# Two transformer blocks on one core: one modulation group summed on VectorE during the input projection, smaller bias rows, and another order of the attention copies

## The chip, the cores and the metric

The kernel runs on one core of a Trainium2 chip. The metric is device time in microseconds (us) of one execution, the median of several runs. All tensors are float32.

## The reference, cut to what matters

Batch is 1, there are 256 tokens and the model width is 1024. `first_block` is a transformer block with two kinds of attention and a gated feed-forward; `second_block` is a Hyena and HGRN mixer followed by a mixture of 16 experts, whose 403 MB of weights are read once. The change lies in the first block:

```python
mod = (silu(c) @ w_ada + b_ada)                 # (1, 6144): a 1024 x 6144 matrix times one vector
shift1, scale1, gate1, shift2, scale2, gate2 = split(mod, 6)
hn = rms_norm(h, norm1_g) * (1 + scale1) + shift1
proj = hn @ w_in                                # 1024 x 3072: q, k, v of both attentions
qa, ka, qb, kb = rms_norm of each head of 64
s = q @ k.T * Dh**-0.5 + bias[rel]              # bias: 12 heads, by relative distance key - query
o = softmax(s) @ v                              # 8 windowed heads, 4 differential heads (p1 - lam * p2)
h = h + gate1 * (o @ w_out)
hn = rms_norm(h, norm2_g) * (1 + scale2) + shift2   # then the feed-forward, gated by gate2
```

## The kernel before

The program is written engine by engine (`block.sync`, `block.gpsimd`, `block.scalar`, `block.vector`, `block.tensor`). Each engine runs its list in the order of the text, and semaphores join them (`reached` and `again` are waits on shared semaphores). Weights stream through `ring`, eight slots of 1 MB. SyncE (SP) issues the load of unit n as soon as unit n-7 is used up (`unit_done`), so the order of `units_of()` is the order of the weights: 8 units `ada` (first third of `w_ada`), 12 units `win` (`w_in`), 16 units `ada` (the other two thirds), 4 units `wout`, and so on.

**Modulation.** A unit `ada` is a 128 x 2048 tile of `w_ada`. `mod_products(m)` (L1720) makes four matmuls of it with the 32 times repeated silu(c) as weights; eight units make one group of 2048 values: group 0 is shift1 and scale1, group 1 gate1 and shift2, group 2 scale2 and gate2. ScalarE copies a finished group out of PSUM (`copy_mod_rows`, L688), TensorE turns it into columns (`mod_columns`, L1741) and VectorE adds `b_ada` (`first_mods`). The second block's modulation is made in another way: GpSimd loads tiles into the arena (`ada_load`, L595), VectorE adds them up scaled by silu(c) (`ada_sum`: the first by a `tensor_scalar`, L1292, the others by a `scalar_tensor_tensor`, L1294), and `mod_fold` sums the result over the partitions with four matmuls.

**First projection** (about 35 to 139 us). TensorE multiplies the 12 units `win` (L1775, L1786, about 7 us each). Between them lie the Hyena filters' spectra (L1764, L1765), which need `filter_halves` (L1102, L1104) on VectorE, and the norms of the heads: `sum_heads`, `head_inverse` (L1110, L1111), ScalarE's root, `spread_heads` (L1803), `head_scales` (L1119). `unmask_bias` (L1092) adds the window mask to the bias tiles just before the last `head_scales`. The bias tiles come from `t12`, 12 rows of 512 values: SP stores each row 128 times in a DRAM scratch (L518), and ScalarE's queue loads them back skewed, a row shifted by one for each partition (L755). Vector instructions stand here in the order `head_inverse(0)`, `head_scales(0)`, `filter_halves(0)`, `filter_halves(1)`, `head_inverse(1)`, `unmask_bias`, `head_scales(1)`.

**Attention** (about 139 to 185 us), 16 pairs p: two windowed heads for 128 queries each (p below 8) or the two maps of one differential head. Each engine has its own loop over p:

```python
# TensorE                      # VectorE                 # ScalarE
scores(p + 2)      # L1851     pair_inverse(p)           two Exp of pair p          # L774
mod_products(10+p) # L1720     pair_max(p + 2) # L1164   (p > 8) scale of p - 1     # L780
turn_probs(p)      # L1864     pair_out(p - 2) # L1187   copy of turned p - 2       # L787
pv(p - 1)          # L1878, L1874                        (some p) mod rows, context squares # L762
```

There are two buffers for scores and exponentials, but one PSUM bank for the turned probabilities (`PTB`) and one tile for the outputs (`PVB`): `turn_probs(p)` waits for ScalarE's copy of p-1, and `pv(p-1)` for VectorE's `pair_out(p-2)`. `mod_products(8)` and `(9)` stand ahead of the loop and `(10)` to `(23)` in its first 14 steps. Then follow `w_out`, the feed-forward (a seven-product scheme with sums on GpSimd and VectorE), the second block's mixers, and the experts.

Of the kernel before, what the change touches and what calls it, by code (L numbers as in the profile page):

```python
# [91 lines left out]
         "up_copied": ("qk_raw", 8), "ada2_landed": ("counts_landed", 16)}  # L92
# [3 lines left out]
def units_of():  # L96

    u = [("ada", i) for i in range(8)] + [("win", i) for i in range(12)] + [("ada", i) for i in range(8, 24)]
    u += [("wout", i) for i in range(4)] + [("ada2", m) for m in NORM2_FILL]
    for i in range(FT // 2):  # L100
        u += [("wup", i)] + ([("cin", CTX_U[0])] if i == FT // 2 - 1 else []) + [("wup", FT // 2 + i)]
        u += [("ada2", m) for m in WUP_FILL.get(i, ())]
    for i in range(FT // 2):
        u += [("wdn", i)]
        u += [("cin", CTX_U[CTX_FILL[i]])] if i in CTX_FILL else []
    u += [("ada2", m) for m in NORM3_FILL]
    u += [("win2", i) for i in WIN2]
    u += [("wout2", i) for i in range(4)]
    return u
# [119 lines left out]
def two_blocks_kernel(nc, a, out):  # L229

    rel_dram = nc.dram_tensor("rel_scratch", (12, P, 512), F32).ap()
# [17 lines left out]
    with ctx:  # L249
# [63 lines left out]

        awide, asum = (at(8, 2048), at(16, 2048), at(0, 2048)), at(82, 2048)
# [50 lines left out]
        def mod_rows(g):  # L365

            if g == 0:
                return X[:, 1, :], HI[:, 1, 0, :]
            return (L[:, 2, :], modrA) if g < 3 else (X[:, 1, :], modrB)
# [112 lines left out]
        def _(sp):  # L482
# [16 lines left out]
            for n, (kind, i) in enumerate(units):  # L499
                if n >= RING:  # L500
                    sp.wait_ge(S["unit_done"], n - RING + 1)
                if kind == "wdn":
                    src = a["w_down"].rearrange("l (k p) n -> p (l k) n", p=P)[:, 2 * i:2 * i + 2, :]
                    dst = slot(n).rearrange("p (k n) -> p k n", k=2)
                elif kind in ("ada", "ada2"):
                    q, k = i // KT, i % KT
                    src = a[UNIT_SRC[kind]][0, k * P:k * P + P, 2048 * q:2048 * q + 2048]
                    dst = slot(n)
                else:
                    src = a[UNIT_SRC[kind]][i, :, :]  # L510
                    dst = slot(n)
                sp.dma_start(dst, src).then_inc(S[f"slot{n % RING}_landed"], 16)
                if n == upos[("wdn", 1)] + RING:
                    sp.wait_ge(S["ffn_act"], FT // 2)
                    expert_pair(0)
                if n == 16:
                    out_of_bank(sp, "rel")
                    sp.dma_start(rel_dram, t12[0:12, :].unsqueeze(1).broadcast_to([12, P, 512])).then_inc(S["rel_stored"], 16)  # L518
# [40 lines left out]
        def _(pool):  # L559
# [10 lines left out]
            load(hc[:, :, :], a["p_ctx"], "ctx_landed")  # L570
# [8 lines left out]

            pool.wait_ge(S["rel_stored"], 16)  # L580
# [4 lines left out]

            pool.wait_ge(S["scores_done"], 16)
# [65 lines left out]
        def _(act):  # L652
# [26 lines left out]
            def copy_mod_rows(g):  # L679

                if g == 4:
                    act.wait_ge(S["ada_folded"], 1)
# [49 lines left out]
            for i in range(12):  # L732
# [19 lines left out]
                if i == 7:  # L752
                    act.wait_ge(S["rel_stored"], 16)
                    act.wait_ge(S["qk_ready"], 4)
                    act.dma_start(biasW[:, :, :], bass.AP(tensor=rel_dram.tensor, offset=P, ap=[[511, P], [512 * P, 12], [1, T + P]])  # L755
                                  ).then_inc(S["bias_landed"], 16)

            def context_squares(i):

                act.wait_ge(S["unit_done"], upos[("win", 11)] + 1)  # L760
                act.wait_ge(S["ctx_landed"], 16)
                sq = A(hn[:, 2 * i:2 * i + 2, :], hc[:, 2 * i:2 * i + 2, :], ACT.Square)  # L762
                if i == 3:
                    sq.then_inc(S["ctx_sq"], 1)

            NP_ = 16
            for p in range(NP_ + 2):
# [20 lines left out]
                if p in (6, 15):  # L788
                    copy_mod_rows(1 if p == 6 else 2)
# [200 lines left out]
        def _(dve):  # L990
# [98 lines left out]
            def unmask_bias():  # L1089
                dve.wait_ge(S["bias_landed"], 16)  # L1090
# [3 lines left out]
            def filter_halves(o):  # L1094
                for i, h in ((0, HR), (2, HI)):
# [8 lines left out]
                    done(V.tensor_tensor(h[:, o, 1, :], e_, o_, ALU.subtract), "lin_emptied_by_dve")  # L1104

# [176 lines left out]
            def ada_sum(j):  # L1282
# [5 lines left out]
                if k == 0 and j:  # L1288
                    dve.wait_ge(S["ada_folded"], 1)
# [216 lines left out]
            dve.wait_ge(S["masks_landed"], 16)  # L1506
# [47 lines left out]
            dve.wait_ge(S["router_landed"], 16)  # L1554
# [98 lines left out]
        def _(pe):  # L1653
# [54 lines left out]
            def mod_products(m):  # L1708
# [5 lines left out]
                if m in (0, 8):  # L1714
                    pe.wait_ge(S["cond_repeated"], 1 if m == 0 else 3)
                if k == 0 and g >= 1:
                    pe.wait_ge(S["mod_rows_copied"], g)
# [6 lines left out]
            def mod_fold(g):  # L1724

                pe.wait_ge(S["ada_summed"], KT if g == 4 else len(SUMMED))
                pe.wait_ge(S["mod_rows_copied"], g)
                for c in range(4):
                    last = MM(mod_rows(g)[0][32 * c:32 * c + 32, :], ones[:, 0:32], asum[:, c * 512:c * 512 + 512],
                              start=True, stop=(g == 4), skip_group_check=True)  # L1730
# [433 lines left out]
            pe.wait_ge(S["dft_landed"], 16)  # L2164
# [244 lines left out]
```

## Time and profile before

| | us |
|---|---|
| median of 3 runs | 1596.08 (1594.73 to 1596.18) |
| profiled execution, its own time | 1595.4 |
| its span | 1593.6 |
| busy in it: TensorE / VectorE / ScalarE / GpSimd | 1230.3 / 435.8 / 223.5 / 143.7 |

A page of the profile gives the busy time of each engine, the same in 40 slices of the span, the chain of work that ended last (followed back from the last instruction, each step to what released it), and groups of instructions by line. The trace behind it can be asked for stretches of time, for one tile, and for who waited for whom. PE is TensorE (PEld its weight loads), DVE VectorE, ACT ScalarE, POOL GpSimd, SP SyncE; SPq, ACTq and POOLq rows are issues of DMAs. Times of rows count from the start of the span.

### The profile page before, as it was taken

The numbers are of one execution on the slowest core, as the hardware profiler recorded it, in microseconds if no ns is written. First come the engines' busy times: TensorE is split into PE (matmuls) and PEld (weight loads), VectorE is DVE, ScalarE is ACT, GpSimd is POOL, SyncE is SP. The second block draws the span as 40 slices with busy tenths as digits, with TensorE's granted clock in tenths as the row PEclk, the third lists the DMA queues.
The fourth block names the chain that finished last, engine by engine and source line by source line (L and its number), as shares of the span: only waits on it lengthen the run. The fifth ranks groups of instructions, "written<-read, shape, count | busy, mean of one in ns | idle before, by whom it ended". The sixth has DMA issues, their size and how long they took to land.

```text
span 1593.6 us, 17838 instructions
## 1 busy us (share of the span) xinstructions
PE 1230.3 (77%) x7618; PEld 691.6 (43%) x7618; DVE 435.8 (27%) x894; ACT 223.5 (14%) x458; POOL 143.7 (9%) x143
## 2 busy tenths in 40 slices
PE   7999999999999999987665655555566666666555
PEld 4775579998888789842111111111111111111111
DVE  4635756775443577320000000000000000000001
ACT  2224522232103321120000000000000000000001
POOL 1100046650000031000000000000000000000000
PEclk9999999999999999999888897888886887788888
DMA  9886765457953335789999999999999999999997
GB/s 387 234 269 267 304 264 212 170 175 304 411 180 132 132 110 186 312 343 428 428 429 428 428 430 427 429 428 428 429 427 429 429 428 429 427 429 428 428 428 299
DMA packets 53414, 545.29 MB, mean 342 GB/s; under 512 B 5884, under 2 KB 7932, under 8 KB 14300
## 3 DMA queue, kind: packets, MB, share of 16 engines
q1 hardware_dynamic: 47724, 521.69, 80.8%
q0 software_dynamic: 3200, 18.43, 2.9%
q10 hardware_dynamic: 2416, 4.07, 0.7%
q8 instruction: 60, 0.98, 0.2%
q14 instruction: 14, 0.11, 0.0%
HBM read 539.97 MB, written 4.19 MB: 341 GB/s over the span
## 4 chain that ended last, share of the span: by engine, by line
PE 50%; DMA 40%; another core or an unknown queue 4%; DVE 3%; ACT 1%; issue 1%; SPq 0%; ACTq 0%; DVEq 0%
DMA arena<-in_exp_w_dram 22%; DMA ring<-in_exp_w_dram 12%; PE L L1936 8%; PE L L2101 7%; DMA tok<-in_exp_w_dram 6%; PE X L2320 6%; PE L L2048 5%; PE L L1775 4%; PE X L2348 3%; PE X L1995 3%; PE L L1786 2%; PE L L2220 2%; PE L L1921 2%; PE L L1720 1%; PE L L2361 1%
## 5 line engine op out<-in xcount | busy, mean ns | idle before, releaser
L2320 PE MATMUL X<-arena,side 128*32 128x512 f32 x1280 | 193.1, 734 | 123.6 <-DMA arena<-in_exp_w_dram 123.6
L2320 PEld LDWEIGHTS X<-arena,side 128*32 128x32 f32 x1280 | 39.7, 122 | 269.7 <-DMA arena<-in_exp_w_dram 195.7
L1609 DVE TENSOR_TENSOR side<-side,X 128x512 f32<-128x512 f32 x16 | 11.0, 687 | 496.8 <-ACT side L972 496.8
L2320 PE MATMUL X<-ring,side 128*32 128x512 f32 x512 | 82.9, 779 | 66.4 <-DMA ring<-in_exp_w_dram 66.4
L2348 PE MATMUL X<-ring,side 128*32 128x512 f32 x512 | 75.9, 721 | 53.2 <-DMA ring<-in_exp_w_dram 53.2
L2101 PE MATMUL L<-tok,ring 128*128 128x256 f32 x448 | 99.4, 379 | 0.3 <-ACT tok L808 0.3
L2101 PEld LDWEIGHTS L<-tok,ring 128*128 128x128 f32 x448 | 84.3, 190 | 13.9 <-issue 3.1
L642 POOL TENSOR_TENSOR side<-side 128x256 f32<-128x256 f32 x16 | 9.8, 615 | 871.0 <-DVE side L1619 808.2
L1614 DVE TENSOR_TENSOR side<-X,side 128x512 f32<-128x512 f32 x16 | 11.1, 692 | 281.0 <-PE X L2348 281.0
L972 ACT ACTIVATE side<-X 128x512 f32<-128x512 f32 x16 | 9.6, 597 | 513.3 <-PE X L2320 513.3
L2048 PE MATMUL L<-arena,ring 128*128 128x256 f32 x352 | 77.4, 379 | 0.3 <-DVE arena L1349 0.3
L2320 PEld LDWEIGHTS X<-ring,side 128*32 128x32 f32 x512 | 16.0, 126 | 130.5 <-DMA ring<-in_exp_w_dram 101.2
L2048 PEld LDWEIGHTS L<-arena,ring 128*128 128x128 f32 x352 | 66.6, 190 | 9.7 <-DVE arena L1349 0.7
L2348 PE MATMUL X<-tok,side 128*32 128x512 f32 x256 | 44.3, 806 | 32.9 <-DMA tok<-in_exp_w_dram 32.9
L2348 PEld LDWEIGHTS X<-ring,side 128*32 128x32 f32 x512 | 15.7, 124 | 115.8 <-DMA ring<-in_exp_w_dram 88.4
L1936 PE MATMUL L<-arena 128*128 128x128 f32 x528 | 63.3, 275 | 1.4 <-DVE L L1320 1.2
L1936 PEld LDWEIGHTS L<-arena 128*128 128x128 f32 x528 | 61.0, 192 | 1.8 <-DVE L L1320 1.4
L2348 PE MATMUL X<-arena,side 128*32 128x512 f32 x256 | 49.1, 907 | 11.9 <-ACT side L976 7.6
L1775 PE MATMUL L<-tok,ring 128*128 128x256 f32 x256 | 56.6, 381 | 0.7 <-ACT tok L700 0.7
L1775 PEld LDWEIGHTS L<-tok,ring 128*128 128x128 f32 x256 | 48.3, 190 | 10.4 <-issue 3.1
L970 ACT ACTIVATE side<-X 128x256 f32<-128x256 f32 x16 | 6.1, 383 | 312.7 <-PE X L2294 312.7
L2361 PE MATMUL L<-side 64*128 64x512 f32 x128 | 38.9, 731 | 13.9 <-DVE side L1614 13.9
(399 smaller groups left out, 1652.9 us busy)
## 6 DMA issues: line engine op xcount, KB each, us to landing
arena<-in_exp_w_dram SPq DMA_DIRECT2D x96, 2048.0 KB, 50.2
ring<-in_exp_w_dram SPq DMA_DIRECT2D x64, 2048.0 KB, 50.1
ring<-in_w_in_dram SPq DMA_DIRECT2D x34, 1024.0 KB, 5.1
more<-in_exp_w_dram SPq DMA_DIRECT2D x15, 2048.0 KB, 49.7
tok<-in_exp_w_dram SPq DMA_DIRECT2D x15, 2048.0 KB, 49.1
ring<-in_w_ada_dram SPq DMA_DIRECT2D x24, 1024.0 KB, 9.3
ring<-in_w_up_dram SPq DMA_DIRECT2D x22, 1024.0 KB, 4.9
arena<-in_ada_w_dram POOLq DMA_DIRECT2D x15, 1024.0 KB, 9.8
```

The lines of the kernel that those rows point to most:

```text
L1720: last = MM(mod_rows(g)[0][32 * c:32 * c + 32, :], cond, slot(n)[:, c * 512:c * 512 + 512], start=(k == 0), stop=(k == KT - 1), skip_group ...
L1775: last = MM(L[:, j % 4, m * T:m * T + T], w[:, k, m * P:m * P + P], src(k), start=(k == 0), stop=(k == KT - 1))
L1786: last = MM(L[:, j % 4, t * T:t * T + T], src[:, k, t * P:t * P + P], w[:, k, :], start=(k == 0), stop=(k == KT - 1))
L1921: last = MM(L[:, j % 4, m * T:m * T + T], w[:, k, m * P:m * P + P], oT[:, k, :], start=(k == 0 and m == 0), stop=(k == KT - 1), skip_group ...
L1936: last = MM(out, w[:, k, :], x(k), start=(first and k == 0), stop=True, skip_group_check=True)
L1995: last = MM(bank[:, x * T:x * T + T], wk, hk, start=(k == 0), stop=(k == KT - 1))
L2048: return MM(L[:, pos["wdn"][m // 2] % 4, (m % 2) * T:(m % 2) * T + T], w[:, kk, m * P:m * P + P], aT[:, 2 * i + kk, :], start=(i == 0 and ...
L2101: last = MM(L[:, j % 4, x * T:x * T + T], wk, hk, start=(k == 0), stop=(k == KT - 1))
L2220: last = MM(L[:, j % 4, m * T:m * T + T], w[:, k, m * P:m * P + P], yTh[:, k, :] if k < HG else yTg[:, k - HG, :], start=(k == 0 and m == ...
L2320: last = MM(X[CAP * j:CAP * j + CAP, w, :], xe[:, k % 2, k // 2, :], v, start=(k == 0), stop=(k == KT - 1))
L2348: last = MM(X[CAP * b:CAP * b + CAP, 2, :], hTe[:, 2 * x + c, CAP * j:CAP * j + CAP], w[:, nb * 512:nb * 512 + 512], start=(u == 16), stop ...
L2361: MM(XB[2 * t + n], ge[h0:h0 + HD, t, :], ys[h0:h0 + HD, :], start=False, stop=True, skip_group_check=True).then_inc(S["scatter_done"], 1)
```

## The change

Eight units `ada`, those of group 1, leave the ring. GpSimd's queue loads them during the first projection into free parts of the arena and of `more`, and VectorE adds them up with silu(c) into `hc` (where the context was loaded before). One fold of four matmuls takes the place of group 1's 32 at the start of the attention, and group 2's eight products stand in the even steps of TensorE's loop only. The context is loaded later, after the fold. The scratch rows are stored 32 times, and ScalarE's queue issues four loads of 32 partitions each. `pair_out(p-2)` moves ahead of `pair_max(p+2)`. Copying and turning group 1 move to steps 2, 4 and 7. Groups 1 and 2 have PSUM banks of their own. Four semaphores are used twice, which only changes counts in other waits (left out below).

```diff
-    u = [("ada", i) for i in range(8)] + [("win", i) for i in range(12)] + [("ada", i) for i in range(8, 24)]
+    u = [("ada", i) for i in range(8)] + [("win", i) for i in range(12)] + [("ada", i) for i in range(16, 24)]
...
-    rel_dram = nc.dram_tensor("rel_scratch", (12, P, 512), F32).ap()
+    rel_dram = nc.dram_tensor("rel_scratch", (12, 32, 512), F32).ap()
...
+        first_wide = (more[:, 256:2304], at(8, 2048), at(78, 2048), more[:, 256:2304], at(20, 2048), at(32, 2048), more[:, 256:2304], at(40, 2048))
+        first_sum = hc.rearrange("p k t -> p (k t)")
...
             pool.wait_ge(S["slot7_landed"], 16)
-            load(hc[:, :, :], a["p_ctx"], "ctx_landed")
+            def first_load(j):
+                pool.dma_start(first_wide[j], a["w_ada"][0, j * P:j * P + P, 2048:4096]).then_inc(S[f"first{j % 4}_landed"], 16)
+            for j in range(3):
+                first_load(j)
             load(dftE[:, :, :, :], a["k_dft"][:, 0:2, :, :], "dftE_landed")
             load(cntW[:, :], a["k_logcnt"], "counts_landed")
...
+            again(pool, "first_summed", 1)
+            first_load(3)
+            reached(pool, "filt_ready")
+            first_load(4)
             pool.wait_ge(S["rel_stored"], 16)
...
+            again(pool, "first_summed", 4)
+            first_load(6)
+            pool.wait_ge(S["HF_done"], 8)
+            pool.wait_ge(S["HN_done"], 2)
+            first_load(5)
+            first_load(7)
+            pool.wait_ge(S["ada_folded"], 1)
+            load(hc[:, :, :], a["p_ctx"], "ctx_landed")
             pool.wait_ge(S["scores_done"], 16)
...
+                if u == 4:
+                    again(act, "first_summed", 2)
                 A(qk[:, u, :, :].rearrange("p m t -> p (m t)"), L[:, j % 4, :], ACT.Copy).then_inc(S["qk_raw"], 1)
...
                 if i == 7:
                     act.wait_ge(S["rel_stored"], 16)
                     act.wait_ge(S["qk_ready"], 4)
-                    act.dma_start(biasW[:, :, :], bass.AP(tensor=rel_dram.tensor, offset=P, ap=[[511, P], [512 * P, 12], [1, T + P]])
-                                  ).then_inc(S["bias_landed"], 16)
+                    again(act, "first_summed", 3)
+                    for g in range(4):
+                        act.dma_start(biasW[32 * g:32 * g + 32, :, :],
+                                      bass.AP(tensor=rel_dram.tensor, offset=P - 32 * g, ap=[[511, 32], [512 * 32, 12], [1, T + P]])
+                                      ).then_inc(S["bias_landed"], 16)
...
-                if p in (6, 15):
-                    copy_mod_rows(1 if p == 6 else 2)
+                if p in (2, 15):
+                    copy_mod_rows(1 if p == 2 else 2)
...
+            def first_add(n):
+                j = (0, 1, 2, 3, 4, 6, 5, 7)[n]
+                again(dve, f"first{j % 4}_landed", 16 * (j // 4 + 1))
+                if n:
+                    again(dve, "first_summed", n)
+                    done(V.scalar_tensor_tensor(first_sum, first_wide[j], csil[:, j:j + 1], first_sum, ALU.mult, ALU.add), "first_summed")
+                else:
+                    done(V.tensor_scalar(first_sum, first_wide[j], csil[:, j:j + 1], None, ALU.mult), "first_summed")
...
             head_inverse(0)
+            for j in range(3):
+                first_add(j)
             head_scales(0)
             filter_halves(0)
+            first_add(3)
+            first_add(4)
             filter_halves(1)
+            for n in range(5, KT):
+                first_add(n)
             head_inverse(1)
             unmask_bias()
             head_scales(1)
...
+                if p >= 2:
+                    pair_out(p - 2)
                 if p + 2 < 16:
                     pair_max(p + 2)
-                if p >= 2:
-                    pair_out(p - 2)
-                if p == 11:
+                if p == 7:
                     first_mods(1)
...
-            mod_products(8)
-            mod_products(9)
+            mod_fold(1)
+            mod_products(16)
             for p in range(17):
                 if p + 2 < 16:
                     scores(p + 2)
-                if p < 14:
-                    mod_products(10 + p)
+                if p < 14 and p % 2 == 0:
+                    mod_products(17 + p // 2)
                 if p < 16:
                     turn_probs(p)
-                if p == 8:
+                if p == 4:
                     mod_columns(1)
```

## Rows read from the trace of the kernel before

**Rows 1.** The page: the chain that ended last, by engine

```profile
PE 50%; DMA 40%; another core or an unknown queue 4%; DVE 3%; ACT 1%; issue 1%; SPq 0%; ACTq 0%; DVEq 0%
```

**Rows 2.** Stretches: length, busy PE, PEld, DVE, ACT, POOL (instructions), clock, DMA share, GB/s

```profile
109.00:122.00 13.00, 13.00 (x62) 11.45 (x61) 0.15 (x1) 2.15 (x4) 0.00 (x0) 1.00 0.90 335
150.00:161.00 11.00, 11.00 (x96) 5.16 (x96) 7.30 (x36) 6.54 (x22) 0.00 (x0) 1.00 1.01 423
```

**Rows 3.** The chain through the attention: start, us, what

```profile
138.83 1.06 PE X L1851 x8
...
148.40 0.59 PE L L1864 x4
148.98 0.59 PE L L1878 x8
149.58 0.63 PE X L1851 x4
150.21 1.00 PE L L1720 x8
...
173.64 0.37 PE L L1864 x2
174.02 0.68 PE L L1874 x4
...
184.84 3.69 PE L L1921 x16
```

**Rows 4.** The timeline of one step, windowed heads: start, us, engine, line

```profile
149.51 0.70 PE L1851 MATMUL X<-arena 64*128 64x256 f32 x4
...
150.26 0.42 DVE L1164 CUSTOM_DVE_ANT_0 arena<-X,arena 128x256 f32<-128x256 f32 x1 [0.91 <-PE X L1851]
...
151.27 0.51 ACT L774 ACTIVATE arena<-arena,small 128x256 f32<-128x256 f32 x1 [1.24 <-DVE small L1167]
...
152.27 0.57 ACT L787 ACTIVATE arena<-L 128x512 f32<-128x512 f32 x1
```

**Rows 5.** The same timeline in the differential heads: ScalarE's end of a step

```profile
172.48 0.36 ACT L787 ACTIVATE arena<-L 128x256 f32<-128x256 f32 x1
...
172.75 0.62 ACT L762 ACTIVATE tok<-tok 128x512 f32<-128x512 f32 x1
```

**Rows 6.** The timeline of VectorE in the first projection, with the idle time before each

```profile
80.90 3.35 DVE L1111 RECIPROCAL arena<-arena 128x512 f32<-128x512 f32 x1
91.66 2.72 DVE L1119 SCALAR_TENSOR_TENSOR arena<-arena,small,X 128x512 f32<-128x512 f32 x4 [7.42 <-PE X L1803]
...
106.15 0.69 DVE L1102 TENSOR_TENSOR side<-L,side 128x512 f32<-128x512 f32 x1 [8.97 <-ACT side L708]
...
127.07 0.69 DVE L1110 TENSOR_SCALAR arena<-X 128x512 f32<-128x512 f32 x1 [17.92 <-PE X L1796]
...
131.06 3.29 DVE L1092 TENSOR_TENSOR arena<-arena 128x3072 f32<-128x3072 f32 x1
135.31 2.72 DVE L1119 SCALAR_TENSOR_TENSOR arena<-arena,small,X 128x512 f32<-128x512 f32 x4 [0.95 <-PE X L1803]
```

**Rows 7.** The arena's groups on VectorE, 370 to 500 us: ns min/median/max, starts

```profile
L1294 DVE SCALAR_TENSOR_TENSOR arena<-arena,small x13: 2350/2352/2353, 378.4 to 437.5; 128x2048 f32<-128x2048 f32 x13
...
L1292 DVE TENSOR_SCALAR arena<-arena,small x2: 1281/1284/1286, 377.0 to 416.0; 128x2048 f32<-128x2048 f32 x2
```

**Rows 8.** DMA issues: what, queue, count, KB each, median us to landing

```profile
arena<-in_ada_w_dram POOLq DMA_DIRECT2D x15, 1024.0 KB, 9.8
...
arena<-rel_scratch ACTq DMA_DIRECT2D x1, 2304.0 KB, 12.6
```

**Rows 9.** GpSimd and SyncE around the bias store, from their timelines

```profile
95.65 0.40 POOL L582 COPY arena<-small 128x256 f32<-128x256 f32 x1 [37.76 <-DMA rel_scratch<-arena]
...
47.95 0.94 SPq L518 DMA_DIRECT2D rel_scratch<-arena  x1
```

**Rows 10.** Waits of TensorE on the input weights, 34 to 140 us: us, times, longest

```profile
PEld L L1775 <- DMA ring<-in_w_in_dram: 1.0, 1, 1.0
```

More of the change, by code:

```diff
@@ L91 @@
          "up_top": ("qk_inv", 2), "up_right": ("max_ready", 16), "up_corner": ("qk_ready", 8),
-         "up_copied": ("qk_raw", 8), "ada2_landed": ("counts_landed", 16)}
+         "up_copied": ("qk_raw", 8), "ada2_landed": ("counts_landed", 16), "first0_landed": ("ctx_landed", 0), "first1_landed": ("router_landed", 0),
+         "first2_landed": ("masks_landed", 0), "first3_landed": ("dft_landed", 0), "first_summed": ("xT_done", 4)}
 CHAIN_OF = {step: chain for chain, steps in CHAINS.items() for step in steps}
 def units_of():
-    u = [("ada", i) for i in range(8)] + [("win", i) for i in range(12)] + [("ada", i) for i in range(8, 24)]
+    u = [("ada", i) for i in range(8)] + [("win", i) for i in range(12)] + [("ada", i) for i in range(16, 24)]
     u += [("wout", i) for i in range(4)] + [("ada2", m) for m in NORM2_FILL]
@@ L368, in mod_rows @@
                 return X[:, 1, :], HI[:, 1, 0, :]
-            return (L[:, 2, :], modrA) if g < 3 else (X[:, 1, :], modrB)
+            return (L[:, 4 - g, :], modrA) if g < 3 else (X[:, 1, :], modrB)
         csil = small[:, 0:8]
@@ L517, in _ @@
                     out_of_bank(sp, "rel")
-                    sp.dma_start(rel_dram, t12[0:12, :].unsqueeze(1).broadcast_to([12, P, 512])).then_inc(S["rel_stored"], 16)
+                    sp.dma_start(rel_dram, t12[0:12, :].unsqueeze(1).broadcast_to([12, 32, 512])).then_inc(S["rel_stored"], 16)
             sp.wait_ge(S["y_nat"], 1)
@@ L679, in copy_mod_rows @@
             def copy_mod_rows(g):
-                if g == 4:
-                    act.wait_ge(S["ada_folded"], 1)
+                if g in (1, 4):
+                    act.wait_ge(S["ada_folded"], 1 if g == 1 else 2)
                 else:
@@ L754, in _ @@
                     act.wait_ge(S["qk_ready"], 4)
-                    act.dma_start(biasW[:, :, :], bass.AP(tensor=rel_dram.tensor, offset=P, ap=[[511, P], [512 * P, 12], [1, T + P]])
-                                  ).then_inc(S["bias_landed"], 16)
+                    again(act, "first_summed", 3)
[3 more added lines that the diff above has]
+                                      ).then_inc(S["bias_landed"], 16)
             def context_squares(i):
                 act.wait_ge(S["unit_done"], upos[("win", 11)] + 1)
-                act.wait_ge(S["ctx_landed"], 16)
+                act.wait_ge(S["ctx_landed"], 48)
                 sq = A(hn[:, 2 * i:2 * i + 2, :], hc[:, 2 * i:2 * i + 2, :], ACT.Square)
@@ L1089, in unmask_bias @@
             def unmask_bias():
-                dve.wait_ge(S["bias_landed"], 16)
+                dve.wait_ge(S["bias_landed"], 64)
                 dve.wait_ge(S["counts_landed"], 16)
@@ L1288, in ada_sum @@
                 if k == 0 and j:
-                    dve.wait_ge(S["ada_folded"], 1)
+                    dve.wait_ge(S["ada_folded"], 2)
                 c_ = csil2[:, k, 0:1]
@@ L1505, in _ @@
             dve.wait_ge(S["lat_gates"], 4)
-            dve.wait_ge(S["masks_landed"], 16)
+            dve.wait_ge(S["masks_landed"], 48)
             V.tensor_tensor(flat(ksum), flat(uA[0]), flat(uB), ALU.add)
@@ L1553, in _ @@
             done(last, "hgrn_ready")
-            dve.wait_ge(S["router_landed"], 16)
+            dve.wait_ge(S["router_landed"], 48)
             V.tensor_tensor(rwg[:, :, :], rw[:, :, :], gain[:, 4, :].unsqueeze(2).broadcast_to([P, KT, 32]), ALU.mult)
@@ L1713, in mod_products @@
                 landed(pe, n)
-                if m in (0, 8):
+                if m in (0, 16):
                     pe.wait_ge(S["cond_repeated"], 1 if m == 0 else 3)
                 if k == 0 and g >= 1:
-                    pe.wait_ge(S["mod_rows_copied"], g)
+                    pe.wait_ge(S["mod_rows_copied"], 1 if g == 2 else g)
                 cond = (cond1a if g == 0 else cond1b if g < 3 else cond2)[:, k, :]
@@ L1724, in mod_fold @@
             def mod_fold(g):
-                pe.wait_ge(S["ada_summed"], KT if g == 4 else len(SUMMED))
+                if g == 1:
+                    again(pe, "first_summed", KT)
+                else:
+                    pe.wait_ge(S["ada_summed"], KT if g == 4 else len(SUMMED))
                 pe.wait_ge(S["mod_rows_copied"], g)
+                total = first_sum if g == 1 else asum
                 for c in range(4):
-                    last = MM(mod_rows(g)[0][32 * c:32 * c + 32, :], ones[:, 0:32], asum[:, c * 512:c * 512 + 512],
-                              start=True, stop=(g == 4), skip_group_check=True)
+                    last = MM(mod_rows(g)[0][32 * c:32 * c + 32, :], ones[:, 0:32], total[:, c * 512:c * 512 + 512],
+                              start=True, stop=(g != 5), skip_group_check=True)
                 last.then_inc(S["ada_folded"], 1)
@@ L2163, in _ @@
             pe.wait_ge(S["ctx_emptied"], NCTX)
-            pe.wait_ge(S["dft_landed"], 16)
+            pe.wait_ge(S["dft_landed"], 48)
             out_of_bank(pe, "hynat", 1)
```

## The prediction

> **What bounds the kernel now.** I read the chain that ended last first. Half of it is TensorE and two fifths are DMA [rows 1]: the DMA part is the stream of expert weights at the end, whose bytes the change doesn't touch. Everything ahead of it is a chain of TensorE stages, and the load orders of the experts hang on steps of that chain. So a microsecond won or lost before the stream moves the stream's start and the end by about one microsecond. The change reaches two stages.
>
> The attention runs from 138.83 to 184.84 us, 46.0 us, and the chain through it is TensorE's nearly alone [rows 3]. One step with windowed heads is scores 0.63, products 1.00, turn 0.59 and output product 0.59 us, 2.81 together; a step with a differential head has 0.37 and 0.68 for the last two, 2.68 together [rows 3]. In the stretch from 150 to 161 us TensorE is busy for all of its 11.0 us, VectorE for 7.30 and ScalarE for 6.54 [rows 2]. So TensorE is the bound, but the others are not far off: about two thirds busy. The DMA engines are full there too (share 1.01, 423 GB/s) [rows 2], which is the ring refilled at one unit for each step.
>
> The first projection is TensorE's as well: its wait for input weights is one of 1.0 us [rows 10]. VectorE has long idle times there: 7.42 us before `head_scales(0)`, 8.97 before `filter_halves(1)` and 17.92 before `head_inverse(1)`. But its last three instructions before the attention are tight: `head_inverse(1)` starts at 127.07, `unmask_bias` ends at 134.35, and `head_scales(1)` starts at 135.31 after 0.95 us idle and ends at 138.03, 0.8 us before the first scores [rows 3, 6]. `head_inverse(1)` can start 0.95 + 0.8, about 1.75 us, later at no cost; behind that every us costs one.
>
> **Attention: the products removed.** Of 16 units' products 8 go, and one fold of the same four matmul shapes comes in: `mod_products(8)` and `(9)` ahead of the loop become fold and `(16)`, no change, and the loop loses its seven odd ones. If TensorE stayed the bound, that is 7 x 1.00 = 7.0 us [rows 3]. It doesn't stay the bound, because a step without products has only 1.81 us of work on TensorE, and `turn_probs(p+1)` waits for ScalarE's copy of p, which stands behind the exponentials of p+2, which wait for the maxima of the scores of p+2. That chain can be read in one step: scores start at 149.51, the maxima at 150.26, the exponentials at 151.27, the copy at 152.27 and takes 0.57 [rows 4]. So the copy is ready 2.76 + 0.57 = 3.33 us after the scores began, and with 0.05 to 0.15 us for the signal (150.26 follows the end of the scores at 150.21 by 0.05 [rows 3, 4]) the next turn can start at 3.45. Turn and output product add 0.59 + 0.59. From the start of a step to the end of the next that is at least 4.63 us. TensorE's own work for one even and one odd step is 2.81 + 1.81 = 4.62, so both limits meet; I take 4.70, because VectorE (two steps of its work are about 3.8 by its two thirds of 2.81 each [rows 2, 3]) has to begin each maximum behind the inverse before it and loses a little. Before, two steps were 5.61: 0.91 won for two windowed steps, four times, 3.6 us.
>
> With differential heads ScalarE has the scale of p-1 as well; its copy starts at 172.48, and the scores of that step began one step of 2.68 before 171.95 (estimate: 169.27), so the copy is done 3.57 after them, the turn starts at 3.70, and 0.37 + 0.68 end at 4.75 [rows 3, 5]. Before it was 5.37, so 0.6 for p = 8 and 9. For p = 10 to 13 the context's squares of 0.62 stand on ScalarE [rows 5], which then has about 2.4 us a step: two steps take 4.85, 0.5 won. Steps 12 and 13 win nothing: 12 keeps its products, and after them the pairs are a chain over VectorE and ScalarE as before. Sum 3.6 + 0.6 + 0.5 = 4.7. Off goes the copy of group 1's rows, 0.6 us on ScalarE, which moves from step 6, where it had cover, to step 2, where it stands in the chain just told, and TensorE's four turns of step 4 (0.4) by the same reason; some of both is hidden, I take 0.4 off. **4.3 us won.** From both sides: 7.0 if TensorE stays the bound; 2 if each pair of steps costs 5.2 and not 4.7, that is if the signals are 0.3 and not 0.1 us.
>
> **The output copies moved.** `pair_out(p-2)` frees the tile that `pv(p-1)` writes. In a step without products `pv(p-1)` can start 1.22 us after the scores, and in the old order the copy would only begin behind the maxima (0.75 + 0.9 us), 0.7 too late. Ahead of the maxima it waits for `pv(p-2)`, which ends as the scores of p+2 begin, so the maxima, which need those scores, wait for nothing new. Its cost is nil, and its gain is in the 4.3.
>
> **VectorE's sums in the projection.** One of 1.28 and seven of 2.35 us [rows 7], 17.7 us in all, go into idle times. The first three (6.0 us and signals) go into the 7.42: they end near 90.4, `head_scales(0)` starts at 91.66 [rows 6]. ScalarE's first copy into the second tile's place comes after the second sum, at about 90.6 against 87.9. Sums 4 and 5 (4.7) go into the 8.97 after `filter_halves(0)` ended near 97.2, if their tiles are there. The loads are issued when the first sum is done, 85.6; a load of this kind takes 9.8 to land [rows 8], so 96 and 98. Ends near 102.3, wanted by 106.15. The last three go into the 17.92: tile 6 is issued near 100 and there in time; 5 and 7 are issued only when the last spectrum has read what they overwrite, near 108.5. Beside them the bias is loaded (12.6 [rows 8]), so tile 5 lands at 118 to 121 and 7 at 122 to 127, and the last sum ends at 124.4 to 129.4. Against 127.07 with 1.75 of slack that costs 0 to 0.6; I take 0. The three first tiles (issued at 31 us) put 2 MB more beside `w_in` than the context did; at the 423 GB/s of full DMA engines [rows 2] that delays later units by 5 us at most, and TensorE takes a unit only every 7 us with one wait so far. I take 0, and 1 at worst.
>
> On the queues: GpSimd's has nothing behind the new waits but the repeated conditioning (needed at 140), the context (needed at step 10, issued at about 142, 10 us) and the loads behind `scores_done`. ScalarE issues three more DMAs where it has idle time. SP's order is unchanged, only eight units shorter, so that 8 MB leave the attention's full DMA stretch; nothing waited for them.
>
> **The bias.** The store writes a quarter. It was issued at 47.95 and done at 95.65 [rows 9]; nobody on the chain waited for it, so the gain is nil, though POOL's new loads now pass that wait at once. The load becomes four of 32 partitions with the same bytes. It was issued at about 109.3, landed after 12.6 us, and is wanted at 131.06 [rows 6, 8]: 9 us of cover and 1.75 of slack. Bounds: 12.6 again, or, at the store's pace (3072 KB in at most 47.7 us [rows 9], from 12 partitions), 2304 KB in 36 us. It is nearer to the first: the bytes go to all partitions in the end and 32 are more than 12. I take 12 to 18 us and no cost. The Trainium skill speaks against this edit (SBUF — State Buffer, Door 1: The DMA port swizzle): a transfer onto partitions 0 to 31 reaches 8 of the 16 ports, with an asymptote of 218 and not 436 GB/s. No row here has a 32-partition load of this size; by that rule the four in a row would take twice as long, and the sum would be 4.3 less the second rival's loss.
>
> **Sum.** 1595.4 - 4.3 = 1591.1 on the profiled execution's own time. The median lies 0.7 above that (1596.08), so I predict 1591.8 for the median. A measurement of this kernel can tell about 0.2%, 3.2 us, from no change; the forecast is just beyond it.
>
> **Rivals.**
> 1. TensorE stays the bound in the attention: 7.0 us, 1589.1. For it: both limits met at 4.62 and 4.63. Against: ScalarE's squares and scale, and the moved row copy.
> 2. The projection ends late. If the bias load takes twice 12.6, it lands at 134.5, 3.4 after 131.06, less 1.75 of slack: 1.7 lost, 1593.5. A seventh tile at 131 costs the same.
> 3. Slower: the four loads go at the store's pace. Landing at 109.3 + 36 = 145.3, 14.2 late, less 1.75: 12.5 lost, less 4.3 won, 1604. It decides from a load of 27.8 us (loss equal to gain); slower by over 0.2% from 31 us. Against it: 335 GB/s moved in that stretch [rows 2] with one such load of all partitions.
> 4. The products were cover: the copy chain is longer than read (5.2 for two steps), 2 won, 1594.1. For it: ScalarE and VectorE at two thirds already.
>
> **Chances.** Forecast (3 to 5.5 won) 0.56; rival 1 0.12; rival 2 0.13; rival 4 0.13; rival 3 0.06. The range leaves out rival 3 and the far ends: 1588.8 to 1595.5. Faster by over 0.2% takes rival 1, nearly all of the forecast and a third of rivals 2 and 4: 0.72. Slower by over 0.2%: 0.06. Within: 0.22.
>
> **What would show it.** In the profile after: scores of every second step 4.7 us apart; the first wait of `turn_probs` on ScalarE's copy in odd steps; 39 to 43 us from the first scores to `w_out`; L1110 at about 127; `head_scales(1)` at 135.3; the bias landed by 128; seven sums of 2.35 us. I am wrong if the stages behind the attention take more than before, or if the first scores are later than 139.

## The result and the profile after

The changed kernel takes 1600.55 us in the median (1598.28 to 1602.43, 6 runs) beside 1595.19 for the kernel before: a ratio of 1.0031, 95% interval 1.0020 to 1.0042. In a second comparison (e11 below) it was 1598.36, ratio 1.0026 (1.0017 to 1.0035). Both intervals lie above 1: the changed kernel is slower, by 5.4 and 2.9 us, where 1591.8 us was predicted and the range ended at 1595.5.

The page of the changed kernel (span, busy times, the chain by engine; its profiled execution took 1599.97 us):

```profile
span 1598.2 us, 17745 instructions
...
PE 1232.0 (77%) x7562; PEld 691.2 (43%) x7562; DVE 453.9 (28%) x902; ACT 222.8 (14%) x458; POOL 150.8 (9%) x151
...
PE 47%; DMA 43%; DVE 4%; another core or an unknown queue 3%; ACT 2%; issue 1%; SPq 1%; ACTq 0%; DVEq 0%
```

VectorE is busy 18 us longer, which are the sums. Of the chain, TensorE's share is smaller and those of DMA and VectorE are larger than in [rows 1]. To see where, here is the chain of the changed kernel from the last spectra to `w_out` (start, us, what; `scores` is L1896 now, the fold L1774, products L1761, `w_out` L1966):

```profile
110.86 26.89 DMA arena<-rel_scratch
137.78 3.37 DVE arena L1117
141.17 2.73 DVE arena L1154 x4
143.94 2.08 PE X L1896 x8
146.02 1.58 PE L L1774 x8
147.61 0.86 PE L L1761 x8
...
184.26 0.41 PE L L1909 x2
184.67 0.85 PE L L1919 x4
185.52 0.85 PE L L1786 x4
186.37 0.87 PE L L1919 x4
187.26 0.30 DVE arena L1228
187.84 5.53 PE L L1966 x16
...
195.52 24.17 PE L L1966 x112
```

A bias load is now a link of the chain. The first of the four was issued at 109.13; the last was issued at 110.86 and landed 26.9 us later, at 137.75, which is 28.6 us after the first issue. The single load of the kernel before took 12.6 [rows 8]. `unmask_bias` (L1117) waited for it, the first scores started at 143.94 and not 138.83 [rows 3]: 5.1 us late. And they took 2.08 us for the 1.06 of before. The granted clock says why (stretches; the columns are those of rows 2):

```profile
136.00:140.00 4.00, 2.69 (x13) 2.03 (x11) 2.23 (x1) 0.60 (x1) 0.00 (x0) 1.00 0.46 133
140.00:144.00 4.00, 0.06 (x2) 0.06 (x2) 3.86 (x5) 0.00 (x0) 0.00 (x0) 0.97 0.60 236
144.00:148.00 4.00, 4.00 (x24) 1.64 (x24) 2.40 (x13) 1.77 (x7) 0.04 (x1) 0.60 0.02 4
148.00:152.00 4.00, 3.43 (x29) 1.33 (x22) 2.45 (x12) 2.14 (x8) 0.49 (x1) 1.00 0.67 231
...
180.00:184.00 4.00, 1.89 (x14) 1.42 (x12) 2.79 (x12) 3.31 (x11) 1.07 (x2) 1.00 0.86 338
184.00:188.00 4.00, 3.17 (x16) 2.82 (x16) 1.12 (x5) 0.91 (x3) 0.00 (x0) 0.59 0.98 397
188.00:192.00 4.00, 4.00 (x11) 3.20 (x12) 3.64 (x1) 2.02 (x3) 0.00 (x0) 0.55 0.08 31
```

TensorE was idle for 5.25 us before the first scores and then ran at 0.60 of its clock: mostly the lower level, 1.2 of 2.4 GHz. The clock fell again at the end of the attention (0.59 and 0.55), behind a stretch in which TensorE had been busy for 1.89 of 4 us.

The start of `w_out`'s last 112 instructions serves as the end point of an account: it is 195.52 here and 190.68 before, 4.84 us later. In the chain of the kernel before, the two products and the entry at that point are:

```profile
139.89 1.85 PE L L1720 x16
...
190.68 24.17 PE L L1921 x112
```

The parts are:

- late scores: +5.1;
- slow first scores, fold and products: +1.6 (2.08 + 1.58 + 0.86 against 1.06 and the 1.85 that the two products took);
- slow last steps: +0.9 (0.85 + 0.85 + 0.87 for the last three entries of L1919 and L1786, which take 0.55 + 0.44 + 0.70 where the clock is full, in e3 and e11 below);
- slow first part of `w_out`: +1.8 (5.53 against 3.69 [rows 3]);
- the attention's removed work: -4.6, measured by itself in e3 below.

The sum is 4.8, and the whole span is 4.6 longer, so behind this point little changed.

### The profile page after: what moved, and what is told of

It reads as the page before. It is cut to its first block, busy times and chain, and to the rows that moved or that the text cites. A ratio compares the mean times of both kernels' runs of the same rounds, so it can differ in the third digit from the quotient of the medians.

```text
span 1598.2 us, 17745 instructions
## 1 busy us (share of the span) xinstructions
PE 1232.0 (77%) x7562; PEld 691.2 (43%) x7562; DVE 453.9 (28%) x902; ACT 222.8 (14%) x458; POOL 150.8 (9%) x151
## 4 chain that ended last, share of the span: by engine, by line
PE 47%; DMA 43%; DVE 4%; another core or an unknown queue 3%; ACT 2%; issue 1%; SPq 1%; ACTq 0%; DVEq 0%
DMA arena<-in_exp_w_dram 19%; DMA ring<-in_exp_w_dram 12%; DMA tok<-in_exp_w_dram 9%; PE L L1981 8%; PE L L2146 7%; PE X L2365 6%; PE L L2093 5%; PE X L2393 3%; PE L L1820 3%; PE X L2040 3%; PE L L1966 2%; PE L L2265 2%; DMA arena<-rel_scratch 2%; DMA ring<-in_w_ada_dram 2%
## 5 line engine op out<-in xcount | busy, mean ns | idle before, releaser
L2365 PE MATMUL X<-ring,side 128*32 128x512 f32 x512 | 89.8, 837 | 69.6 <-DMA ring<-in_exp_w_dram 69.6
L2393 PE MATMUL X<-ring,side 128*32 128x512 f32 x512 | 77.9, 736 | 54.2 <-DMA ring<-in_exp_w_dram 54.0
L2365 PEld LDWEIGHTS X<-ring,side 128*32 128x32 f32 x512 | 16.8, 132 | 136.3 <-DMA ring<-in_exp_w_dram 104.9
L2406 PE MATMUL L<-side 64*128 64x512 f32 x128 | 35.4, 672 | 13.9 <-DVE side L1655 13.9
## 6 DMA issues: line engine op xcount, KB each, us to landing
ring<-in_w_ada_dram SPq DMA_DIRECT2D x16, 1024.0 KB, 10.6
```

Source lines behind the costliest of these rows:

```text
L2365: last = MM(X[CAP * j:CAP * j + CAP, w, :], xe[:, k % 2, k // 2, :], v, start=(k == 0), stop=(k == KT - 1))
L2393: last = MM(X[CAP * b:CAP * b + CAP, 2, :], hTe[:, 2 * x + c, CAP * j:CAP * j + CAP], w[:, nb * 512:nb * 512 + 512], start=(u == 16), stop ...
L2406: MM(XB[2 * t + n], ge[h0:h0 + HD, t, :], ys[h0:h0 + HD, :], start=False, stop=True, skip_group_check=True).then_inc(S["scatter_done"], 1)
```

## The experiments

In all of them "landed" counts from the first of the four issues to the last landing, since that is what `unmask_bias` waits for. The runs were made on three chips: e1 to e4 on one, e5 to e8 on the second, e9 to e11 on the third. The ratios compare each with the kernel before on the same chip, whose medians were 1595.16, 1595.52 and 1595.45 us.

**e1: one load again.** The scratch rows are stored 128 times and loaded at once; the sums stay.

```diff
-rel_dram = nc.dram_tensor("rel_scratch", (12, 32, 512), F32).ap()
+rel_dram = nc.dram_tensor("rel_scratch", (12, P, 512), F32).ap()
-for g in range(4): act.dma_start(biasW[32 * g:32 * g + 32, :, :], ...)
+act.dma_start(biasW[:, :, :], bass.AP(..., offset=P, ap=[[511, P], [512 * P, 12], [1, T + P]]))
```

> The changed kernel with the bias part undone: rows stored 128 times and one load of all 128 partitions. Theory A (loads onto 32 neighbouring partitions are slow): the load lands 13 to 17 us after its issue, unmask_bias starts at 131, the first scores at 139 and not 144, and the median is 1590 to 1593. Theory B (the load is slow because tiles 5 and 7 are loaded beside it): it lands 20 us or more after its issue here too, the first scores are after 142, and the median stays above 1597. Theory C (it is slow because four loads read the same 32 rows in DRAM): as A.

Measured: 1602.20 us, ratio 1.0041 (1.0027 to 1.0055): slower still, but for another reason. GpSimd, VectorE and TensorE in its timelines:

```profile
103.77 0.40 POOL L594 COPY arena<-small 128x256 f32<-128x256 f32 x1 [16.70 <-DMA rel_scratch<-arena]
...
107.78 2.35 DVE L1135 SCALAR_TENSOR_TENSOR tok<-more,small,tok 128x2048 f32<-128x2048 f32 x1 [10.56 <-DMA more<-in_w_ada_dram]
...
116.31 1.87 PE L1808 MATMUL L<-arena 128*1 128x512 f32 x2 [9.07 <-DVE side L1127]
```

The 3 MB store was not done until 103.8. VectorE waited 10.56 us for the fourth tile and 2.57 us more for the fifth, which was issued at 86.5 and landed at 112.7. Both sums stand ahead of `filter_halves(1)` on VectorE, and the last spectrum waited 9.07 us for that. The bias load, issued at 118.3 behind this stall, took 26.7 us although it was one load onto all partitions. So this run doesn't part A and C from B as it was meant to, because it brought a stall of its own, and with it more company for the load: 4.7 MB of the ring and 2.2 MB of tiles moved between 118 and 145 us. It shows something else: the sums need the smaller store. The prediction called the store's gain nil; that held for the kernel before only.

**e2: the bias part alone, on the kernel before.**

> The kernel before with the bias part alone: rows stored 32 times, four loads of 32 partitions, and no sums on VectorE. Theory A and theory C: the last of the four lands 20 to 27 us after the first issue, at 129 to 136, and the time is 1595 to 1600. Theory B: it lands 13 to 15 us after, and the time is that of the kernel before, 1595.

Measured: 1595.51 us, ratio 1.0002 (0.9993 to 1.0012). Landed after 16.8 us, between the 13 to 15 of theory B and the 20 to 27 of A and C. That is at 127.2, ahead of the 132.2 at which this execution wanted it. Four loads onto 32 neighbouring partitions cost about 4 us more than the one, and by themselves nothing of the time.

**e8: the changed kernel without 2 MB beside the bias.** Tiles 5 and 7 are loaded 8 columns wide, so the sum lacks most of them; the instructions stay.

```diff
-            first_load(5)
-            first_load(7)
+            for j in (5, 7):
+                pool.dma_start(first_wide[j][:, 0:8], a["w_ada"][0, j * P:j * P + P, 2048:2056]).then_inc(S[f"first{j % 4}_landed"], 16)
```

> The changed kernel with tiles 5 and 7 loaded only 8 columns wide (the sum then lacks most of these two tiles; all instructions of VectorE stay). The four bias loads are as in the changed kernel, onto 32 neighbouring partitions each, but now without 2 MB beside them. If the slow load needs both (neighbouring partitions and the tiles beside it), the last of the four lands 12 to 16 us after the first issue, first scores at 139, 1590 to 1593. If the layout alone or the shared rows in DRAM did it: 24 to 28 us, 1598 to 1602.

Measured: 1591.57 us, ratio 0.9980 (0.9970 to 0.9989). Landed after 16.6 us, just above the 12 to 16 expected if it takes both; `unmask_bias` started at 130.8 and waited for nothing.

**e4: every fourth partition.** The tiles are whole again, and each load goes to partitions g, g+4, g+8 and so on.

```diff
-act.dma_start(biasW[32 * g:32 * g + 32, :, :], bass.AP(..., offset=P - 32 * g, ap=[[511, 32], [512 * 32, 12], [1, T + P]]))
+act.dma_start(biasW[g:P:4, :, :], bass.AP(..., offset=P - g, ap=[[508, 32], [512 * 32, 12], [1, T + P]]))
```

> The changed kernel with each of the four loads going to every fourth partition (g, g+4, g+8 and so on) and not to 32 neighbouring ones; same bytes, same rows in DRAM, same number of descriptors. Theory A: landed by 17 us after the first issue, first scores at 139, time 1590 to 1593. Theories B and C: 24 to 28 us, as in the changed kernel, time 1598 to 1602.

Measured: 1593.14 us, ratio 0.9983 (0.9973 to 0.9992). Landed after 19.4 us (the last was issued later, at 113.7, and took 16.7), near 130.4 and in time for `unmask_bias` at 132.8. That is 2.4 us above theory A's 17 and well below the 24 to 28 of B and C. Issues of e4, then of the changed kernel, as median us to landing of the four:

```profile
arena<-rel_scratch ACTq DMA_DIRECT2D x4, 576.0 KB, 14.0
```

```profile
arena<-rel_scratch ACTq DMA_DIRECT2D x4, 576.0 KB, 22.1
```

All cases of the load:

| landed after, us | without tiles 5 and 7 | with tiles 5 and 7 | one unit earlier |
|---|---|---|---|
| 32 neighbouring partitions | 16.8 (e2), 16.6 (e8) | 28.6 (changed kernel) | 27.2 (e3) |
| every fourth partition | not run | 19.4 (e4) | 15.1 (e5) |
| one load of 128 partitions | 12.6 (before) | 26.7 (e1, in more company) | not run |

Theory C falls, since e4 and e8 read the same 32 rows. Of A and B neither alone is enough here: without the tiles, or with the spread layout beside them, the load was in time. In the changed kernel's place the neighbouring form was 9 us slower than the spread one, and these 9 us are more than the slack.

What the layout costs by itself can be read from the profile's line of ScalarE's queue (q10), which carries nothing but the bias load between 95 and 145 us: packets, MB, and the time that the packets took as a share of the time of all 16 DMA engines. In this order: the kernel before, e2, the changed kernel, e4.

```profile
q10 hardware_dynamic: 1552, 2.36, 13.3%
```

```profile
q10 hardware_dynamic: 1600, 2.36, 22.5%
```

```profile
q10 hardware_dynamic: 1600, 2.36, 21.3%
```

```profile
q10 hardware_dynamic: 1600, 2.36, 13.0%
```

The same 2.36 MB held the engines for 6.5 to 7.2 us of these 50 when the partitions were spread (e4, e5) or all 128 (before, e1), and for 10.1 to 11.4 us when they were neighbours (e2, e3, e8, changed kernel), with the tiles beside them or not. So the neighbouring layout makes the load 1.4 to 1.7 times as much work for the engines. The company then decides how long the engines take to get through it: they are fully busy until the load is done, at a low rate:

```profile
110.00:122.00 12.00, 12.00 (x57) 10.56 (x56) 3.93 (x3) 1.20 (x3) 0.07 (x1) 1.00 1.02 281
122.00:136.00 14.00, 14.00 (x71) 10.49 (x70) 6.10 (x3) 3.69 (x6) 0.00 (x0) 1.00 1.03 274
```

The kernel before moved 335 GB/s there at a share of 0.90 [rows 2]. The extra work is about 4 us of the 9 between the changed kernel and e4; where the other 5 come from no run shows. And e1 shows that enough company does it without the layout: its load was no more work than before (13.3%) and took 26.7 us. The Trainium skill's port map (SBUF — State Buffer, Door 1: The DMA port swizzle) puts partitions 0 to 31 on 8 of the 16 ports; by the same map every fourth partition reaches all 16. The shares agree in direction. They show less than a halved rate: at most 1.7 times the engines' time, and 16.8 against 12.6 us to landing.

**e3: the bias loads one unit earlier.** After the first filter's spectra, near 98 us, where their place is free.

```diff
-                if i == 7:
+                if i == 6:
                     act.wait_ge(S["rel_stored"], 16)
```

> The changed kernel with the four bias loads issued one unit earlier, after the first filter's spectra (near 98 us) and not after the second's (109). Every theory of the load: with 27 us it lands by 126, before 131, so the first scores are at 139. What is left is the attention part: by the prediction 4.3 us won, median 1590 to 1593. If the changed kernel's attention is itself short of the forecast (43.9 us where 41.7 was forecast) for another reason than the wait before it, 1593 to 1595.

Measured: 1591.71 us (1589.94 to 1594.82), ratio 0.9979 (0.9970 to 0.9988). The load landed at 124.4, after 27.2 us, with tile 6 and the others beside it, and cost nothing. Its chain:

```profile
138.75 0.66 PE X L1896 x4
...
146.31 0.63 PE X L1896 x4
146.94 1.00 PE L L1761 x8
147.94 0.59 PE L L1909 x4
148.53 0.59 PE L L1923 x8
149.12 0.63 PE X L1896 x4
149.75 0.60 PE L L1909 x4
150.35 0.59 PE L L1923 x8
150.95 0.63 PE X L1896 x4
...
180.18 3.69 PE L L1966 x16
```

From scores to scores over two steps it is 4.64 us (146.31 to 150.95; forecast 4.70, before 5.61). From the first scores to `w_out` it is 41.4 us (138.75 to 180.18) where it was 46.0 [rows 3]: 4.6 us won in the attention. Forecast: 4.3. In these windowed steps TensorE doesn't wait at all: `turn_probs` (L1909) starts as the scores end, at 149.75. This profiled execution was the fastest of the eleven runs; the median is 1.8 above it.

**e6: e3 with the output copies behind the maxima, as before the change.**

> The changed kernel with the bias loads one unit earlier, and the output copies back behind the maxima, as before the change. The prediction's working: in a step without products the copy ends about 0.7 us later than the output product could start, so of the six such steps each loses up to 0.7, 2 to 4 us in all, 1593.5 to 1596. Rival: the output product is late by ScalarE's copy of the turned probabilities anyway, and the order is worth nothing: 1591.7 within 0.7.

Measured: 1595.43 us (1593.87 to 1598.40), ratio 1.0001 (0.9992 to 1.0010), 3.7 above e3 and 3.9 above e8, which ran on the same chip (1591.57): the attention part is worth nothing without the moved copy. From the first scores to `w_out` its profile has 46.4 us (140.52 to 186.93), as before the change. The output product (L1923) in a step without products:

```profile
152.45 0.28 DVE L1228 COPY arena<-L 128x128 f32<-128x128 f32 x1
...
152.88 0.66 PE L1923 MATMUL L<-arena 128*64 128x128 f32 x8 [0.77 <-DVE arena L1228]
```

It waits 0.77 us for the copy, where 0.7 was worked out. Part of the loss may be the clock, which this profile shows at 0.71 from 180 to 184 us and at 0.86 over the next 4.

**e7 and e10: TensorE kept busy before the first scores.** The changed kernel with 36 transposes of the identity ahead of the first scores; both runs have the same program. e11 is the changed kernel itself again.

```diff
+            pe.wait_ge(S["lin_emptied_by_act"], emptied[pos["win"][11]][1])
+            keep_busy(L[:, 2, :], 36)
             pe.wait_ge(S["qk_ready"], 8)
```

> The changed kernel with 36 transposes of the identity into a free bank while TensorE waits for the bias before the first scores. Theory: its wait there is followed by a granted clock of 0.60, which made the two first scores take 2.08 us and not 1.06 and the first products 1.58 and not 0.99; with the engine kept busy the clock stays at 1.00, the first scores are still at 144, and 1.5 to 2 us are won: 1598.5 to 1599.5. Rival: the clock falls all the same, or the transposes delay the scores: 1600.5 or more. The low clock at the end of the attention (184 to 192) is not touched by this and may stay.

> The same kernel as the one with 36 transposes before the first scores, for a profile of an execution near its median (1596.4): by the theory the first scores are at 143.9 to 145 us, they take 1.06 us and not 2.08, and no stretch from 144 to 192 us shows a clock below 0.9. By the rival (the low clock at the end of the attention is a matter of its own) the end still shows one.

> The changed kernel itself once more, beside the others on one chip: 1598 to 1602, the last bias load landed 25 to 28 us after the first issue, the first scores at 144 us and the clock at 0.6 behind them.

Measured: e7 1596.39 us, ratio 1.0007 (0.9998 to 1.0016), below the 1598.5 to 1599.5 expected; e10 1596.08, ratio 1.0003 (0.9993 to 1.0014), beside e11's 1598.36, ratio 1.0026 (1.0017 to 1.0035), on one chip. So 2.3 us are won with the bias as late as before, and the two intervals don't overlap. The profiled execution of e10 was the slowest of its runs (1600.41), so there is no trace near the median, for which it was meant. In it the clock behind the wait stays up and the first scores, at 146.22, take as long as before the change; at the end of the attention the clock falls all the same:

```profile
144.00:148.00 4.00, 3.44 (x32) 2.40 (x34) 3.16 (x10) 0.01 (x1) 0.00 (x0) 1.00 0.24 98
...
188.00:192.00 4.00, 3.40 (x8) 2.80 (x9) 3.66 (x4) 2.43 (x3) 0.00 (x0) 0.50 0.17 72
```

e7's profiled execution, the slowest of its runs too (1603.05), shows 0.85 from 144 to 148 us and 0.72 from 148 to 152. Its bias landed at 139.2, and the transposes were over 1.97 us before the scores could start (0.56 us in e10), so they don't hold the clock in every execution. e11's execution (1597.09) is the reverse of e10's: after a wait of 4.87 us the clock is 0.58, and at the end it stays at 1.00:

```profile
144.00:148.00 4.00, 4.00 (x24) 1.08 (x20) 2.58 (x13) 2.08 (x8) 0.51 (x1) 0.58 0.00 0
...
180.00:184.00 4.00, 1.86 (x13) 1.50 (x14) 2.88 (x13) 3.12 (x10) 1.06 (x2) 1.00 0.95 375
184.00:188.00 4.00, 3.35 (x20) 2.77 (x21) 1.95 (x6) 1.95 (x4) 0.00 (x0) 1.00 0.92 371
```

Its bias landed 28.2 us after the first issue, just above the 25 to 28 expected. Its account: first scores at 143.53, 4.7 late; slow scores, fold and products 1.7; less 4.6 won; 1.8 in all, and measured at `w_out` (186.67) 1.8. So the two falls are separate. The first comes with the wait, in both profiles of the changed kernel. The second comes in some executions and is worth about 2.7 us (0.9 + 1.8 above). What brings it isn't shown: TensorE was busy for 1.89 us from 180 to 184 in the execution where the clock fell and for 1.86 in the one where it didn't. Of the profiles with the thinner attention and no filling, e1, e4, e6, e7, e10 and one of the two of the changed kernel have it, and e3, e5, e8 and the other don't. The two profiles with all the products (the kernel before and e2) don't have it either. That fits the thinner work as a cause, but two are too few.

**e5 and e9: both bias edits, and filled steps.** e5 is e3 with e4's layout; e9 is e5 with six transposes of the identity in each of TensorE's steps 9, 11, 13 and 14, of which the first three lost their products (step 14 never had any).

```diff
                 if p < 14 and p % 2 == 0:
                     mod_products(17 + p // 2)
+                elif 9 <= p < 15:
+                    pe.wait_ge(S["mods_ready"], 1)
+                    keep_busy(L[:, 3, :], 6)
```

> The changed kernel with the four bias loads issued one unit earlier and each going to every fourth partition. If the bias is out of the way in the earlier issue alone (first scores at 138.8), this adds nothing: 1591.7 within 1. It can also take the load out of the way of tile 6, which landed at 112 and not 109 there; that is off the path.

> The kernel with the earlier bias loads onto every fourth partition, and six transposes of the identity into a free bank in TensorE's steps 9, 11, 13 and 14, whose products are gone. Theory: the removed products were also work that held TensorE's granted clock; in some executions it falls near the end of the attention (0.77 to 0.86 seen there), and with the steps filled it doesn't: median 1590 to 1591.3, highest of the fast runs below 1592. Rival: the fall is not of those steps, the spread stays 2 to 3 us, and the transposes cost up to 1 us: 1591 to 1592.

Measured: e5 1590.88 us (1590.10 to 1592.92), ratio 0.9973 (0.9963 to 0.9984), landed after 15.1 us. e9 1590.41 us (1590.10 to 1591.37), ratio 0.9970 (0.9959 to 0.9982): the narrowest of all. Both are faster than the kernel before and the changed one. e5 and e9 ran on different chips and their intervals overlap, so that filling wins anything in the median isn't shown. The spread, 1.3 us in 7 runs against 2.8 in 8 of e5 and 4.9 in 11 of e3, goes the way of the theory, but it isn't proof: e5's own profile has the clock at 1.00 without any filling, and the kernel before, with all its products, spreads over 3.2 us in 30 runs on e5's chip (1594.47 to 1597.66).

## Why the prediction was wrong

- **The bias, no cost: this is the step that failed.** "I take 12 to 18 us and no cost", with 36 us as the other bound and a chance of 0.06 for it. It took 28.6. With the layout alone it would have been inside (16.6 and 16.8). The prediction weighed the bias as company for the tiles, with a range for their landing, and forgot the reverse: the tiles are company for the bias. They even landed sooner than forecast (their sums started at 115.44 and 121.70, where 118 to 121 and 122 to 127 were taken), and the bias paid. Its "9 us of cover and 1.75 of slack" were used up, and the first scores came 5.1 us late. That is the loss that rival 3 priced (it was to decide from 27.8 us), but not by its mechanism: alone, the four loads were nowhere near the store's pace of 36 us. Rival 2, twice 12.6 and so 25.2 us, was the nearer one in kind and too small.
- **The clock was in no term.** A wait of TensorE was priced one to one. Here the wait of 5.25 us cost 1.6 more behind it by the clock. With that the late load costs 6.7 us, and 6.65 is the difference between the medians of the changed kernel (e11, 1598.36) and of e3 (1591.71), though from different chips. The fall at the attention's end cost 2.7 more in the profiled execution; that the removed products had held the clock there is a guess that no run settles. In that execution late scores and won attention, 5.1 and 4.6, nearly cancel, and the 4.3 us of the clock are what is left.
- **The bound and the way to the end** were right: the difference of 4.84 us in `w_out` went through to the end as 4.6.
- **Products removed, 4.3 us:** right, 4.6 in e3. The split was a little off. The first eight steps won 2.9 us (forecast 3.6, less the 0.4 taken off), the last eight 1.7 (forecast 1.1); TensorE's four turns of 0.44 moved from the second part to the first and explain most of it. The expected wait on ScalarE's copy isn't there in the windowed steps 2 to 7, which take TensorE's own 4.64 us for two; the two limits, worked out as 4.62 and 4.63, were too close to tell apart.
- **Copies moved:** right in mechanism and size; the 0.7 us is 0.77 in e6, and the whole is 3.7.
- **Sums on VectorE, 0:** right. The last sum ended at 124.05, 0.35 before the forecast 124.4 to 129.4, and `head_inverse(1)` started at 126.93.
- **The smaller store, nil:** wrong as a reading of the change. With the sums in, the full store costs 9 us at the last spectrum (e1).

## What to carry to other kernels

When a change adds transfers beside an existing one, price the existing one again in the new company and in its new shape together, and compare that with its slack; where a load's destination is free earlier, issue it earlier. If four loads must share a tile, try every fourth partition before 32 neighbours: the same bytes held the DMA engines for 6.5 us and not 10.6 here (e4 and the changed kernel). A new wait of TensorE can cost more than its length: here 5.25 us cost 1.6 more, because the instructions behind it ran at the lower clock, and transposes into a free bank during the wait won 2.3 us in the median. And work taken from one engine of a loop of three wins only what the next limit leaves: here some 3.7 of 4.6 us hung on the place of a copy of 0.28 us.

## What the runs showed of the hardware

- Four 0.6 MB loads onto 32 neighbouring partitions each took 16.6 to 16.8 us without the tiles (e8, e2) and 28.6 us beside 2 MB of them; onto every fourth partition 19.4 us beside the same 2 MB (e4). DMA engines were counted as fully busy (1.02) at 281 GB/s.
- The same 2.36 MB took the 16 DMA engines 10.1 to 11.4 us onto 32 neighbouring partitions (20.2 to 22.7% of 50 us, in e2, e3, e8 and the changed kernel) and 6.5 to 7.2 us onto every fourth or all 128 (13.0 to 14.4%, in e4, e5, e1 and the kernel before).
- A store of 3 MB from 12 partitions was under way from 48 to 96 us [rows 9], and to 103.8 us with the first tiles beside it (e1). VectorE then waited 10.56 us for a tile that it had without a wait behind the store of a quarter of the size.
- After 5.25 us of idle time the granted clock of TensorE was 0.60 over the next 4 us, and two steps' scores took 2.08 for 1.06 us; after 4.87 us it was 0.58 (e11). With transposes during the wait it was 1.00 in one execution (e10), and 0.85 and 0.72 over 8 us in another (e7).
- With nearly the same busy time of TensorE (1.89 and 1.86 of 4 us) the clock behind it fell to 0.59 in one execution of the changed kernel and stayed at 1.00 in another.
